# Second expert biases and the last expert's rows as products at the end, and the split of the turned rows on GpSimd, in a transformer block with 32 experts

## The reference

```python
logits = t @ w_router + b_router
top_v, top_i = lax.top_k(logits, 4)           # 4 of 32 experts
top_w = softmax(top_v)
# for every expert e, over the rows xe that chose it:
hh  = xe @ w1[e] + b1[e]                       # 1024 -> 2048
glu = minimum(hh[:, :1024], 7.0); lin = clip(hh[:, 1024:], -7.0, 7.0)
act = glu * sigmoid(1.702 * glu) * (lin + 1.0)
y   = act @ w2[e] + b2[e]                      # 1024 -> 1024
out[token] += y * weight[token, e]
# x = x + out; result = RMSNorm(x) * norm_f_g
```

## Time and profile before

| | |
|---|---|
| median of 3 runs | 1553.04 us (1552.08 to 1553.85) |
| profiled execution, its own time | 1552.45 us |
| its span, first to last instruction | 1550.7 us |
| PE busy (of the span) | 1478.0 us (95%) |
| PE weight loads | 1192.4 us (77%) |
| DVE busy | 1329.0 us (86%) |
| ACT busy | 1117.4 us (72%) |
| POOL busy | 232.8 us (15%) |
| mean granted clock of PE | 0.978 |
| HBM read and written | 445.05 MB and 23.07 MB |

### The profile page before, as it was taken

One profiled execution on the slowest core, in us unless ns is written; L12 is line 12 of the kernel. 1 busy time (PEld: TensorE's weight loads), 2 busy tenths in 40 slices (PEclk: granted clock), 3 DMA queues, 4 the chain that ended last, 5 costly groups with the idle time before them and its releaser, 6 DMA issues.

```text
span 1550.7 us, 22355 instructions
## 1 busy us (share of the span) xinstructions
PE 1478.0 (95%) x7046; PEld 1192.4 (77%) x7046; DVE 1329.0 (86%) x1532; ACT 1117.4 (72%) x1313; POOL 232.8 (15%) x200
## 2 busy tenths in 40 slices
PE   6999998888999999999999999999999999999993
PEld 5788786776778888888888887888888888888872
DVE  5476655477999999999999999999999999999983
ACT  4466554354788888888888888888888888888873
POOL 5000000034011111111111111111111111111110
PEclk9999999988999999999999999999999999999997
DMA  7021121169899999999999999999999999999943
GB/s 235 25 82 41 42 82 55 43 265 362 325 372 360 374 357 360 370 369 365 367 368 364 358 357 368 357 367 365 352 363 371 365 370 362 368 356 367 353 152 124
DMA packets 100214, 451.88 MB, mean 291 GB/s; under 512 B 13504, under 2 KB 25792, under 8 KB 67408
## 3 DMA queue, kind: packets, MB, share of 16 engines
q1 hardware_dynamic: 90704, 434.55, 74.3%
q0 software_dynamic: 9472, 16.85, 4.4%
HBM read 445.05 MB, written 23.07 MB: 302 GB/s over the span
## 4 chain that ended last, share of the span: by engine, by line
PE 91%; DVE 4%; ACT 2%; DMA 1%; issue 1%; POOL 1%; POOLq 0%; SPq 0%; ACTq 0%; DVEq 0%
PE zpair L1885 45%; PE bank L1885 23%; PE bank L1545 4%; PE bank L1546 3%; PE bank L1547 3%; PE bank L1854 2%; PE bank L1860 2%; PE zpair L1617 1%; PE zpair L1869 1%; PE bank L1681 1%; PE bank L1632 1%; PE bank L1878 1%; DVE stage_lo L1079 1%; PE zpair L1605 1%; PE zpair L1653 1%
## 5 line engine op out<-in xcount | busy, mean ns | idle before, releaser
L723 ACT CAST stage_hi<-ring 128x1024 fp32r<-128x1024 f32 x796 | 835.5, 1055 | 222.3 <-PE zpair L1885 150.5
L1079 DVE TENSOR_TENSOR stage_lo<-ring,stage_hi 128x1024 fp32r<-128x1024 f32 x796 | 952.9, 1223 | 48.0 <-ACT stage_hi L723 13.7
L1885 PE MATMUL zpair<-stage_hi,act_hi 128*128 128x512 f32 x1024 | 324.1, 398 | 7.3 <-DVE stage_lo L1079 5.3
L1885 PE MATMUL zpair<-stage_hi,act_lo 128*128 128x512 f32 x1024 | 316.8, 391 | 0.0
L1885 PE MATMUL zpair<-stage_lo,act_hi 128*128 128x512 f32 x1024 | 316.7, 391 | 0.0
L1885 PEld LDWEIGHTS zpair<-stage_hi,act_hi 128*128 128x128 f32 x1024 | 188.0, 189 | 56.0 <-DVE stage_lo L1079 13.6
L1885 PEld LDWEIGHTS zpair<-stage_lo,act_hi 128*128 128x128 f32 x1024 | 193.0, 188 | 41.1
L1885 PEld LDWEIGHTS zpair<-stage_hi,act_lo 128*128 128x128 f32 x1024 | 192.8, 188 | 40.7
L1885 PE MATMUL bank<-stage_hi,act_hi 128*128 128x512 f32 x512 | 162.7, 399 | 0.1
L1885 PE MATMUL bank<-stage_lo,act_hi 128*128 128x512 f32 x512 | 159.4, 393 | 0.0
L1885 PE MATMUL bank<-stage_hi,act_lo 128*128 128x512 f32 x512 | 158.7, 391 | 0.0
(11 more groups left out here) (284 smaller groups left out, 1492.6 us busy)
## 6 DMA issues: line engine op xcount, KB each, us to landing
ring<-in_w SPq DMA_DIRECT2D x384, 1024.0 KB, 7.6
ring<-in_w_in SPq DMA_DIRECT2D x12, 1024.0 KB, 5.4
ring<-in_w_out SPq DMA_DIRECT2D x4, 1024.0 KB, 5.0
xs_all<-in_x SPq DMA_DIRECT2D x4, 512.0 KB, 7.5
ring<-in_x SPq DMA_DIRECT2D x4, 512.0 KB, 3.7
tn_scratch<-qk SPq DMA_DIRECT2D x4, 512.0 KB, 2.7
x_scratch<-ring SPq DMA_DIRECT2D x4, 512.0 KB, 3.8
ring<-x_scratch SPq DMA_DIRECT2D x4, 512.0 KB, 5.2
```

Of the source, the lines that this page charges most:

```text
L723: nc.scalar.copy(dst, src).then_inc(split_hi, 1)
L1079: nc.vector.tensor_tensor(dst, src, hi_ap.bitcast(F32), ALU.subtract).then_inc(split_lo, 1)
L1885: mm = pe.matmul(bank[b0 + h][:], w[:, k, :], m[:, j % STAGES, h * BANK:(h + 1) * BANK], start=False, stop=stop and w is T_lo)
```

## The change

1. The second biases leave the loop. `bias_2`, `select2`, `sel2` and `bias2` are gone; the first product of each second matrix starts the sum (`start=`). PE keeps the waits (`second_free`) and has one more, for `wdT_lo`.
2. In their place POOL makes a dense table of the weights of each token for each expert (five products and sums ahead of the gather of expert 2), three times side by side. In the second expert's body PE turns it (`dense_turn`, four transposes of 96 rows), ACT rounds it and DVE makes the low part of 32 rows. At the end PE multiplies the table with the biases for each tile of tokens (`second_biases`, 96 rows in the contraction: high by high, low by high, high by low).
3. The last expert's rows are not scattered (when there is no overflow): ACT writes them out times their weights, rounded (`last_high`), DVE the rest (`last_low`), and PE adds them to the tiles by products with a one-hot matrix of their tokens (`last_expert`). The residual is loaded once the scatter before has landed and the last piece is split; DVE adds the banks to it (`added`) before ACT squares.
4. The turned rows of experts 2 to 31 are no longer split by ACT and DVE from PSUM. ACT copies them to SBUF in float32 (`x_out`, in the place of `x_evac`), and POOL makes the high part with two copies and the low part with two subtractions of 128x512 (`x_split`, between gather and scatter). POOL's loop over the experts is written out.
5. DVE's first clip moves from behind piece 17 to behind piece 18.

```diff
@@ sync @@
             sp.wait_ge(split_lo, W_IN_PIECES + 8)
             for g in range(4):
                 sp.dma_start(b1raw[32 * g:32 * g + 32, :], ...).then_inc(bias_in, 16)
-                sp.dma_start(b2raw[32 * g:32 * g + 32, :], ...).then_inc(bias_in, 16)
...
             for c in (4, 5):
                 load_w1(0, c, moe_slot(c))
+            for g in range(3):
+                sp.dma_start(b2raw[32 * g:32 * g + 32, :], b2[0]).then_inc(b2_in, 16)
...
+            sp.wait_ge(split_lo, MAIN.split(E - 1, W1P + W2P - 1))
             sp.wait_ge(all_scattered, 1)
             for t in range(TT):
                 sp.dma_start(total(t), x2_d[t * P:(t + 1) * P, :]).then_inc(fin_in[t], 16)
@@ gpsimd @@
+            def x_split(i):
+                pool.wait_ge(xT_out, i - 1)
+                for h in range(2):
+                    nc.gpsimd.tensor_copy(xT_hi[:, 4 * h:4 * h + 4, :], xT_raw[:, 4 * h:4 * h + 4, :]).then_inc(xT_hi_r, 1)
+                pool.wait_ge(xT_hi_r, 2 * i + 2)
+                for h in range(2):
+                    nc.gpsimd.tensor_tensor(xT_lo[:, 4 * h:4 * h + 4, :], xT_raw[:, 4 * h:4 * h + 4, :],
+                                            xT_hi[:, 4 * h:4 * h + 4, :].bitcast(F32), ALU.subtract).then_inc(xT_lo_r, 1)
...
+            dk = dense_k.rearrange("p (t k) e -> p t k e", k=TOPK)
+            step(nc.gpsimd.tensor_tensor(dense_k, oh, w4.unsqueeze(2).to_broadcast([P, 16, E]), ALU.mult))
+            step(nc.gpsimd.tensor_tensor(dk[:, :, 0:2, :], dk[:, :, 0:2, :], dk[:, :, 2:4, :], ALU.add))
+            for r in range(3):
+                nc.gpsimd.tensor_tensor(dense[:, :, r, :], dk[:, :, 0, :], dk[:, :, 1, :], ALU.add).then_inc(dense_r, 1)
             pool.wait_ge(x2_out, 16 * TT)
             gather(2)
-            with pool.Fori(2, E - 1) as i:
+            for i in range(2, E - 1):
                 gather(i + 1)
+                x_split(i)
                 scatter(i - 2)
-            for i in range(E - 3, E):
+            x_split(E - 1)
+            for i in range(E - 3, E - 1):
                 scatter(i)
@@ scalar @@
-            nc.scalar.copy(bias2[:], b2raw).then_inc(bias_hi, 1)
...
+            def x_out(t):
+                act.wait_ge(x_turned, t + 1)
+                act.wait_ge(xT_lo_r, 2 * t)
+                nc.scalar.copy(xT_raw[:, 0:4, :], bank[6][:].rearrange("p (k t) -> p k t", k=4))
+                nc.scalar.copy(xT_raw[:, 4:8, :], bank[7][:].rearrange("p (k t) -> p k t", k=4)).then_inc(xT_out, 1)
...
+                        if j == 14 and first and b == MOE0:
+                            act.wait_ge(dense_mm, 1)
+                            nc.scalar.copy(wdT[0:96, :], bank[4][0:96, :]).then_inc(wdT_hi, 1)
-                        if j == 21 and not last:
+                        if j == 21 and not last and b == MOE0:
+                            x_out(t + 1)
...
+            def last_high(used_at):
+                act.wait_ge(used, used_at)
+                act.wait_ge(weight_ready, E)
+                for h in range(2):
+                    nc.scalar.activation(y_hi[:, h * BANK:(h + 1) * BANK], bank[4 + h][:], ACT.Copy, scale=wcol[:]).then_inc(last_hi, 1)
             run_items(MAIN)
+            act.wait_ge(b2_in, 48)
+            act.wait_ge(dense_mm, 1)
+            nc.scalar.copy(b2r[0:96, :], b2raw[0:96, :]).then_inc(b2_hi, 1)
+            last_high(MAIN.base - OPROJ_PIECES + 24 * E)
...
             for t in range(TT):
-                act.wait_ge(fin_in[t], 16)
+                act.wait_ge(fin_added, t + 1)
@@ vector @@
-                nc.vector.tensor_tensor(bias2[r, :], b2raw[r, :], bias2[r, :].bitcast(F32), ALU.subtract).then_inc(bias_lo, 1)
...
                         if j == 5 and not first:
-                            select2(t - 1, r * 24 + (ub - 8))
                             weights(t - 1)
...
-                        if j == 17:
-                            clip(t, 0, r * 24 + (ub - 8 + W1P))
                         if j == 18:
+                            clip(t, 0, r * 24 + (ub - 8 + W1P))
                             clip(t, 1, None)
-                        if j == 21 and not last:
+                        if j == 21 and not last and b != MOE0:
                             turned_lo(xT_lo, xT_hi, xT_hi_r, xT_lo_r, t + 1)
...
+            dve.wait_ge(last_col, 1)
+            for t in range(TT):
+                nc.vector.tensor_scalar(onehot[:, t * P:(t + 1) * P], iotas[:], float(t * P), last_rows[:], ALU.add, ALU.is_equal).then_inc(onehot_r, 1)
             dve.wait_ge(gf_in, 16)
+            def added(t):
+                dve.wait_ge(fin_in[t], 16)
+                dve.wait_ge(fin_mm, t + 1)
+                for h in range(2):
+                    half = total(t)[:, h * BANK:(h + 1) * BANK]
+                    ins = nc.vector.tensor_tensor(half, bank[FIN[t] + h], half, ALU.add)
+                ins.then_inc(fin_added, 1)
...
+            added(0)
+            added(1)
             for t in range(TT):
+                if t + 2 < TT:
+                    added(t + 2)
                 final(t)
@@ tensor @@
-            def bias_2(t):
-                pe.wait_ge(sel2_r, t + 1)
+            def second_free(t):
                 wait(pe, y_ready, t)
+                pe.wait_ge(wdT_lo, 1)
                 pe.wait_ge(over_ready, 1)
-                for c in range(2):
-                    half = slice(64 * c, 64 * c + 64)
-                    pe.matmul(bank[4 + c][:], sel2[half, :], bias2[half, :], start=True, stop=False)
...
                         if j == 8:
                             turn_a(t - 1)
+                        if j == 10 and first and b == MOE0:
+                            dense_turn()
...
+            def second_biases(t):
+                for h in range(2):
+                    pe.matmul(bank[FIN[t] + h], wdT[0:96, t * P:(t + 1) * P], b2r[0:96, h * BANK:(h + 1) * BANK], start=True, stop=False)
+            def last_expert(t):
+                for m in (y_hi, y_lo):
+                    for h in range(2):
+                        mm = pe.matmul(bank[FIN[t] + h], onehot[:, t * P:(t + 1) * P], m[:, h * BANK:(h + 1) * BANK],
+                                       start=False, stop=m is y_lo)
+                mm.then_inc(fin_mm, 1)
+            pe.wait_ge(b2_lo, 1)
+            for t in range(3):
+                second_biases(t)
+            pe.wait_ge(onehot_r, TT)
+            pe.wait_ge(y_ready, E)
+            for t in range(TT):
+                if t == 3:
+                    second_biases(t)
+                last_expert(t)
```

More of the change, by code:

```diff
@@ L232, in build @@
         bias1 = over("bias1", [P, D], F32R, room_at)
-        bias2 = over("bias2", [P, BANK], F32R, room_at + 4096)
+        wdT = over("wdT", [P, S], F32R, room_at + 4096)
         sel1 = over("sel1", [P, P], F32R, room_at + 6144)
-        sel2 = over("sel2", [P, P], F32R, room_at + 6656)
+        onehot = over("onehot", [P, S], F32R, room_at + 7168)
         sq_sum = [f_sum, f_neg]
@@ L253, in build @@
         b1raw = slot(9)[:, 0:D]
-        b2raw = slot(9)[:, D:D + BANK]
+        b2raw = over("b2raw", [P, D], F32, act_at + 4 * (KT * S + 3 * D))
+        b2r = act_hi[:, 3 * D:4 * D]
+        dense_all = over("dense_all", [P, D], F32, act_at + 4 * 3 * D)
+        dense_k = dense_all[:, 0:512].rearrange("p (a e) -> p a e", e=E)
+        dense = dense_all[:, 512:512 + 3 * TT * E].rearrange("p (t r e) -> p t r e", r=3, e=E)
+        xT_raw = over("xT_raw", [P, KT, P], F32, act_at + 4 * (KT * S + 2 * D))
+        y_hi = act_hi[:, 2 * D:3 * D]
+        y_lo = act_lo[:, 2 * D:3 * D]
         g2b = slot(8)[:, 0:D]
@@ L703, in _, with last_scatter @@
             n_over = pool.value_load(novi[0:1, 0:1], min_val=0, max_val=OVER)
+            def last_scatter():
+                pool.wait_ge(y_ready, E)
+                nc.gpsimd.tensor_copy(sidx[:], gtab[:, E - 1:E]).then_inc(sidx_copied, 1)
+                pool.wait_ge(sidx_copied, E)
+                pool.reg_add(bound, zero, S - 1)
+                for part, done, at in ((y_hi.bitcast(F32), scattered, 16 * E), (y_lo.bitcast(F32), last_lo_out, 16)):
+                    nc.gpsimd.indirect_dma_start(out=x2_d[:, :], out_offset=bass.IndirectOffsetOnAxis(ap=sidx[:, 0:1], axis=0),
+                                                 in_=part, in_offset=None, bounds_check=bound, oob_is_err=False,
+                                                 compute_op=ALU.add).then_inc(done, 16)
+                    pool.wait_ge(done, at)
+                pool.sem_inc(yout_free, 1)
             with pool.If(n_over > 0):
+                last_scatter()
                 gather(E)
@@ L1505, in body @@
                             turned_lo(aT_lo, aT_hi, aT_hi_r, aT_lo_r, t - 1)
-                        if j == 17:
+                        if j == 14 and first and b == MOE0:
+                            dve.wait_ge(wdT_hi, 1)
```

(12 more changed lines are left out.)

55 lines of the change are left out of this document (37 added, 18 removed).

## The result

The changed kernel takes 1576.99 us (median of 4, 1574.24 to 1577.84) against 1553.44 for the kernel before: a ratio of 1.0145, 95% interval 1.0128 to 1.0161. It is slower, by 23.5 us, where 31.6 were forecast (1585.0, range 1542 to 1612). The profiled execution took 1574.24 us with a span of 1572.4, 21.7 more than the span before, and what follows is measured on the spans.

The account below looks back on a forecast made before the run. PE was taken to bound the loop as long as DVE stays ahead. From 1552.45 us, +51 −15.5 −0.6 −3.5 +0.6 −0.1 gave 1584.4, as a median 1585, range 1542 to 1612.

Parts of the forecast that it names:

- The side and the mechanism: Slower, chance 0.77: in the expert loop GpSimd's split and DVE's two-SBUF-input work take turns, pushing DVE 2.7 us an expert.
- +51: Sum of PE's added waits in the expert loop from GpSimd's split: 1.7 us an expert, times 30.
- The second bias: Bias products off PE before the second weights: 0.5 us saved an expert, 15.5 us over 31 experts.
- DVE's lead at piece 2: Piece 2 of the next expert, called the tightest place: DVE's rest ready 0.85 us before PE starts on it.
- What PE waits: PE waits for DVE's pushed rests at pieces 22, 23, 0 and 2: 1.7 us an expert.
- the rival of a starved GpSimd: GpSimd's split waits on DVE, low part some 3 us late: +90, 1624 us; chance 0.10, shared with dear copies.
- The copy: Each GpSimd copy of the turned rows in the split takes 0.6 to 0.7 us.
- The end: After the last products: last expert added by products instead of scatter and reload, saving 3.5 us (2 to 5).
- The last expert's 0.5: Last expert's first product starts earlier without selection and two bias products: 0.6 us saved.
- Once only: Dense table in the second expert: four transposes, a copy and a 32-row subtraction cost 0.6 us of PE.
- First rival: GpSimd's split runs in DVE's gaps in the loop, no wait on PE: 1534 us; chance 0.13.
- the small terms: Last expert's start −0.6 us, dense table once +0.6, fewer bias copies before the router −0.1.

Follow-up runs that it names:

- e3: The changed kernel with GpSimd's four split operations replaced by six memsets, which read nothing from SBUF (zeros in place of the split rows): 1528.19 us.
- e8: e10 plus two spare GpSimd products of 128x512 from two SBUF tiles for each of experts 2 to 30, result unused by PE and DVE: 1568.29 us.
- e9: As e8, but the two spare operations are memsets of 128x1024, which only write: 1534.74 us.
- e1: The changed kernel with the split of the turned rows back on ACT and DVE; biases, end and clip order stay changed: 1541.3 us.
- e6: e1 with DVE's first clip behind piece 17 again, as before the change: 1548.02 us.
- e7: The changed kernel with DVE's first clip behind piece 17 again: 1585.15 us.
- e4: The changed kernel with ACT's copy of the turned rows behind piece 20 instead of 21: 1592.86 us.
- e2: The kernel before with only the split on GpSimd (ACT's copy, loop written out); biases, clips and end as before: 1590.16 us.
- e10: e1 with DVE's low part of the turned rows in two halves, behind pieces 22 and 23, instead of both behind piece 21: 1534.81 us.

## Why the prediction was right

- *The side and the mechanism*: right. DVE and GpSimd take turns by whole instructions: 2.7 us of push an expert were forecast, 2.6 measured. e3, e8 and e9 show that it is this. Against e3, where nobody is held up, the changed kernel takes 49 us more; +51 were forecast.
- *The second bias*: 0.5 taken within 0.43 to 0.67; from the turn to the second piece it is 0.65, near the most. Over 31 experts 4.7 us more than forecast. But that is time off PE's path and not time won: with the work of the split back on ACT and DVE an expert gains 0.28 us with the moved clip (e1) and nothing without it (e6). The prediction took "as long as DVE stays ahead" as given and looked for DVE's lead at piece 2, where piece 22 had 0.18 us.
- *What PE waits*: 1.7 an expert forecast, 0.92 + 0.65 = 1.57 measured (36.95 against 36.03 for an expert, and the bias). 4 us over 30. Two waits an expert came where four were named. But the spread named, "over pieces 22, 23, 0 and 2", was wrong. Pieces 22 and 23 are in time, as ACT's part of piece 22 starts 6.2 us after the turn (644.23) where I had 6.4 and DVE went on at 645.32. The first wait is for GpSimd's low part, which I had only in the rival of a starved GpSimd. Both limits lie close together: e7 and e4 take the one away and PE stands for the other.
- *The copy*: 0.6 to 0.7 taken. In e4 GpSimd's two copies take 1.43 us together, the first behind a rest of DVE; in the changed kernel, beside DVE's rests, 2.62.
- *The end*: 3.5 forecast, 5.7 measured. DVE's chain of additions and scalings was put at 10.8 us; from 1558.88 to 1569.32 it is 10.4, and it starts 5.8 us behind the last products where 6.6 were counted, since PE's granted clock stayed at 1.00 from 1553 to 1562 us and the one-hots, 0.88 for four, ran while PE made the bias products. The last expert's 0.5 was put at 0.6.
- *Once only*: 0.6 forecast. The turn before the second weights of the first body is at 383.64 instead of 383.21. In the next body the four transposes of the dense table hold the next products back by 0.35 us (409.05 to 409.40).
- *First rival*: 1534 forecast if GpSimd's work were absorbed; e3, where it holds nobody up, is 1528.

By the spans 31.9 us were forecast and 21.7 came. Counted so, the two largest terms were off by 4.7 and 3.9 to the same side, the end by 2.2: 10.8 of the 10.2 us, and the small terms give the rest back. What I did not see, and only the misses of e1 and e2 showed, is that piece 22 is the tight place: taking work off PE alone wins little there.

Part of the closeness is luck. The 51 us were reckoned on top of a kernel in which PE waits for nothing, and on top of that they are right (49 by e3). But with the turned rows split by ACT and DVE the rest of the change doesn't give such a kernel: it is worth 12 us (e1 against the kernel before), where the forecast's other terms add up to 19, and the split on top of e1 costs 36, not 51. The wait at piece 22 was left out on both sides, and the two misses, 7 and 15 us, partly cancel.

Open: the kernel before with only the clip moved wasn't run, so e1's 0.28 us an expert are not divided between clip and bias; that PE is busy in all of the 920 us argues that the clip alone wins nothing. And how much of the 5.7 us at the end comes from the products and how much from the sooner reload wasn't tried apart.

## What to carry to other kernels

Before moving work from a busy VectorE to an idle GpSimd, count what each engine reads from SBUF in that stretch: an operation that GpSimd does beside VectorE's with two SBUF inputs is paid in good part by VectorE (2.6 us for the four of the split, 1.18 for the two of e8), and each of its subtractions took 2.20 us instead of 1.29. Here 1.2 us of VectorE work was swapped for 2.6 us of standing, in the stretch where VectorE was least ahead. And when one engine gets shorter, look again where the next one's lead is smallest, at every piece and not only at the one that comes to mind: halving the turned rows' low part over two pieces (e10) won 6.5 us where the change of engine lost 36.

## What the runs showed of the hardware

- A GpSimd memset to SBUF doesn't hold DVE's two-input operations: 0.96 us for 128x1024 in e9 and DVE's rests unchanged. Products of two SBUF tiles do, at 1.16 us an expert for two of 128x512 (e8). A DVE subtraction with one input in PSUM, beside such a product, takes its usual 0.68 us (e8).
- Where GpSimd's subtractions and DVE's rests follow each other without a gap they alternate one by one: DVE's rests go from 1.22 to 2.31 and 2.29 us, GpSimd's subtractions from 1.29 to between 2.14 and 2.25 (all 52 from 560 to 1500 us). This is not so for every operation: GpSimd's index copy of one column, 0.18 us alone, takes 2.48 us before and mostly 3.74 in e1, beside DVE's rests that follow each other every 1.13 us and stay at 1.22.
- PE's stands of 1 us or less in each expert left the granted clock alone: it is 1.00 from 560 to 1480 us in both kernels, though PE is busy for 890 us of the 920 after and for all of them before.
- The gather's issue takes 1.39 us before and 1.05 after. It isn't the loop written out: with that loop, but the first clip behind piece 17, it takes 1.48 (e2, e6 and e7). It goes with the place of the clip; why is not shown.
